# A recurrence's decay sums taken once, with sums, norms and a transposition moved among TensorE's steps

## The reference, cut to what matters

```python
decay = jnp.exp(-jnp.exp(w))
kk = kk * lax.rsqrt(jnp.maximum(jnp.sum(kk * kk, axis=-1, keepdims=True), 1e-24))
k = k * (1 + (a - 1) * k_a)
def step(state, inp):
    r_t, w_t, k_t, v_t, a_t, b_t = inp          # a = -kk, b = kk * a
    sa = jnp.einsum('bhvk,bhk->bhv', state, a_t)
    state = (state * w_t[:, :, None, :] + sa[..., None] * b_t[:, :, None, :]
             + v_t[..., None] * k_t[:, :, None, :])
    y = jnp.einsum('bhvk,bhk->bhv', state, r_t)
    return state, y
```

## Time and profile before

| | us |
|---|---|
| runs of the kernel before, median of 3 | 3309.3 |
| lowest, highest | 3306.87, 3312.51 |
| the profiled execution's own span | 3305.3 |
| TensorE busy in it | 3189.0 (96%) |
| VectorE busy | 2607.8 (79%) |
| ScalarE busy | 1161.1 (35%) |
| GpSimd busy | 2052.8 (62%) |

### The profile page before, as it was taken

One profiled execution on the slowest core, in us unless ns is written; L12 is line 12 of the kernel. 1 busy time (PEld: TensorE's weight loads), 2 busy tenths in 40 slices (PEclk: granted clock), 3 DMA queues, 4 the chain that ended last, 5 costly groups with the idle time before them and its releaser, 6 DMA issues. The chain is left out here.

```text
span 3305.3 us, 57051 instructions
## 1 busy us (share of the span) xinstructions
PE 3189.0 (96%) x21428; PEld 2745.2 (83%) x21428; DVE 2607.8 (79%) x4810; ACT 1161.1 (35%) x1786; POOL 2052.8 (62%) x1304
## 2 busy tenths in 40 slices
PE   8998998899999999999999898999999999999998
PEld 3445887699999999888888777999999998888886
DVE  8583664589998886689899765899988866888997
ACT  0113544233334443333333423333344333333333
POOL 1122444377785655788888603777855568888884
PEclk9999998999999999999999999999999999999999
DMA  9750002377787887999999623777878889999995
GB/s 336 279 207 29 3 4 98 121 255 262 256 280 240 308 323 290 378 348 344 360 352 342 215 83 129 255 265 255 277 249 306 317 296 377 346 347 361 349 342 179
DMA packets 364075, 856.31 MB, mean 259 GB/s; under 512 B 32969, under 2 KB 201393, under 8 KB 355538
## 3 DMA queue, kind: packets, MB, share of 16 engines
q1 hardware_dynamic: 278610, 542.98, 47.3%
q0 software_dynamic: 85248, 310.42, 26.2%
HBM read 750.46 MB, written 102.81 MB: 258 GB/s over the span
## 5 line engine op out<-in xcount | busy, mean ns | idle before, releaser
L1804 PE MATMUL peer_acc<-peer_hhi,peer_uhi 128*128 128x384 f32 x2048 | 697.1, 340 | 8.4 <-POOL peer1same_ulo L2004 4.5
L1804 PE MATMUL peer_acc<-peer_hlo,peer_uhi 128*128 128x384 f32 x2048 | 686.2, 335 | 0.0
L2004 POOL TENSOR_TENSOR peer1same_ulo<-peer_u,peer_uhi 128x1024 fp32r<-128x1024 f32 x128 | 311.7, 2438 | 192.1 <-ACT peer_uhi L1884 190.7
L2004 POOL TENSOR_TENSOR peer0same_ulo<-peer_u,peer_uhi 128x1024 fp32r<-128x1024 f32 x128 | 311.7, 2438 | 191.9 <-ACT peer_uhi L1884 191.1
L1880 ACT ACTIVATE peer_gel<-peer_acc 128x384 f32<-128x384 f32 x256 | 125.7, 491 | 768.9 <-PE peer_acc L1804 768.9
L1804 PEld LDWEIGHTS peer_acc<-peer_hhi,peer_uhi 128*128 128x128 f32 x2048 | 386.3, 189 | 11.4 <-POOL peer1same_ulo L2004 5.8
L1804 PEld LDWEIGHTS peer_acc<-peer_hlo,peer_uhi 128*128 128x128 f32 x2048 | 386.2, 189 | 1.0 <-issue 0.5
L2035 POOL TENSOR_TENSOR peer0lsame_vlo<-peer0l_v,peer0l_vhi 128x1024 fp32r<-128x1024 f32 x128 | 310.3, 2424 | 85.6 <-ACT peer0l_vhi L1919 85.2
L2035 POOL TENSOR_TENSOR peer1lsame_vlo<-peer1l_v,peer1l_vhi 128x1024 fp32r<-128x1024 f32 x128 | 310.2, 2424 | 85.4 <-ACT peer1l_vhi L1919 84.7
L2067 DVE SCALAR_TENSOR_TENSOR peer_acc<-peer_row,peer_p_g,peer_acc 128x1024 f32<-128x1024 f32 x254 | 325.1, 1280 | 36.1 <-DMA peer_row<-in_pe_v,peer_idx 36.1
L1804 PE MATMUL peer_acc<-peer_hhi,peer0same_ulo 128*128 128x384 f32 x1024 | 343.7, 336 | 0.0
(11 more groups left out here) (453 smaller groups left out, 6892.7 us busy)
## 6 DMA issues: line engine op xcount, KB each, us to landing
peer_u<-in_pe_uT SPq DMA_DIRECT2D x256, 512.0 KB, 5.8
peer0l_v<-in_pe_v SPq DMA_DIRECT2D x128, 512.0 KB, 6.0
peer1l_v<-in_pe_v SPq DMA_DIRECT2D x128, 512.0 KB, 6.1
activations<-peer_gel SPq DMA_DIRECT2D x256, 192.0 KB, 6.1
rw_g<-in_ada POOLq DMA_DIRECT2D x60, 512.0 KB, 5.4
routing<-peer0m_wb SPq DMA_DIRECT2D x24, 1024.0 KB, 8.3
peer0l_wt<-routing SPq DMA_DIRECT2D x64, 384.0 KB, 7.5
peer0l_gl<-activations SPq DMA_DIRECT2D x128, 192.0 KB, 7.1
```

The source lines that it names most:

```text
L1804: mm = pe.matmul(ub[e % 2][:, 0:SD], a, h[:, k, 0:SD], start=(n == 0), stop=(n == 3 * KT - 1))
L2004: g.tensor_tensor(ulo[:, q].rearrange("p k e -> p (k e)"), u[:, q].rearrange("p k e -> p (k e)"), uhi[:, e % NH].bitcast(F32).rearrange("p ...
```

## The change

The sums that include the step are kept, 128 columns wide; the exclusive ones are no longer computed. Where AR needs them, ScalarE reads the inclusive ones one column to the left, and a further activation with scale 0 fills the first column. `sum_decay(K, m)` and `spread_norm(K, m)` work on one of the four row tiles; TensorE issues three sums behind level 0 and the fourth inside level 1, between its halves, then three norms behind level 1 and the fourth inside level 2. The transposition b = 1 moves from ahead of level 0 to behind level 3, and ScalarE's copy of it from behind level 0's first copies to behind `decays(K + 1, 1)`. VectorE scales keys and products behind level 2, not level 1. The sums now take bank 3 alone, and the norms bank 2. `cum_done` counts one for a round, and the waits that read it are changed to fit; the waits for `y_done`, `nat_done` and `state_made` in `decays` are as they were.

```diff
--- before
+++ after
@@ -113,7 +113,7 @@
-    for name, n in (("masks", 4 * P), ("sums", 2 * P), ("eye", HALF_P), ("pairs", HALF_P), ("levels", SCAN_LEVELS * HALF_P),
+    for name, n in (("masks", 4 * P), ("sums", P), ("eye", HALF_P), ("pairs", HALF_P), ("levels", SCAN_LEVELS * HALF_P),
@@ -637,7 +637,7 @@
-        cumB = gB[:, 2:4].rearrange("p b (m i q) -> p (b m) i q", m=2, i=2)
+        cumB = gB[:, 3].rearrange("p (m q) -> p m q", q=P)
@@ -689,7 +689,7 @@
-            sp.wait_ge(cum_done, 2 * ROUNDS)
+            sp.wait_ge(cum_done, ROUNDS)
@@ -756,7 +756,7 @@
-                norms = gB[:, 3 if K > 0 else 0].rearrange("p (m q) -> p m q", q=P)
+                norms = gB[:, 2 if K > 0 else 0].rearrange("p (m q) -> p m q", q=P)
@@ -841,7 +841,7 @@
                         invert_deviation(K - 1)
-                    if n == 1 and coming:
+                    if n == 2 and coming:
                         scale_keys(K + 1)
@@ -871,16 +871,17 @@
 
                 r, c, mine = where(K)
                 ms, of = slice(RT // 2 * b, RT // 2 * b + RT // 2), slice(mine.start + RT // 2 * b, mine.start + RT // 2 * b + RT // 2)
-                act.wait_ge(cum_done, 2 * K + (b + 1))
+                act.wait_ge(cum_done, K + 1)
                 if K >= 2:
                     act.wait_ge(y_done, K - 1)
                     act.wait_ge(nat_done, 2 * (K - 1))
                 if K >= 4:
                     act.wait_ge(state_made, K - 3)
-                a.activation(AR[:, of, 0], cumB[:, ms, 1], ACT.Exp, scale=LOG_DECAY, bias=up[:])
-                a.activation(KS[:, of], cumB[:, ms, 0], ACT.Exp, scale=-LOG_DECAY, bias=down[:])
-                a.activation(AR[:, of, 1], cumB[:, ms, 0], ACT.Exp, scale=LOG_DECAY, bias=up[:])
-                a.activation(fac[:, K // 2 % 2, of], cumB[:, ms, 0, P - 1], ACT.Exp, scale=LOG_DECAY).then_inc(exps_made, 1)
+                a.activation(AR[:, of, 0, 0], cumB[:, ms, 0], ACT.Exp, scale=0.0, bias=up[:])
+                a.activation(AR[:, of, 0, 1:P], cumB[:, ms, 0:P - 1], ACT.Exp, scale=LOG_DECAY, bias=up[:])
+                a.activation(KS[:, of], cumB[:, ms], ACT.Exp, scale=-LOG_DECAY, bias=down[:])
+                a.activation(AR[:, of, 1], cumB[:, ms], ACT.Exp, scale=LOG_DECAY, bias=up[:])
+                a.activation(fac[:, K // 2 % 2, of], cumB[:, ms, P - 1], ACT.Exp, scale=LOG_DECAY).then_inc(exps_made, 1)
 
             def take_d(K, n, s):
                 act.wait_ge(d_done, STREAMS * (LV + 1) * K + STREAMS * n + (s + 1))
@@ -911,10 +912,11 @@
                     take_u(K - 1)
+                keeps = past and K - 1 < ROUNDS - 2
                 for s in range(STREAMS):
                     take_d(K, 0, s)
-                    if past and K - 1 < ROUNDS - 2:
-                        take_nat(K - 1, s)
+                    if keeps and s == 0:
+                        take_nat(K - 1, 0)
                 for n in range(LV):
@@ -924,6 +926,8 @@
                         decays(K + 1, 0)
                     if n == 3 and coming:
                         decays(K + 1, 1)
+                    if n == 3 and keeps:
+                        take_nat(K - 1, 1)
                     if not coming:
                         for k in range((KT + LV - 1) // LV * n, min((KT + LV - 1) // LV * (n + 1), KT)):
                             round_wo(k)
@@ -953,22 +957,21 @@
 
-            def sum_decays(K, b):
+            def sum_decay(K, m):
 
                 r, c, mine = where(K)
-                for m in range(RT // 2 * b, RT // 2 * b + RT // 2):
-                    n = RT * r + m
-                    mm = pe.matmul(cumB[:, m].rearrange("p i q -> p (i q)"), rw["s"][:, c, n * P:(n + 1) * P], held["sums"],
-                                   start=True, stop=True)
-                mm.then_inc(cum_done, 1)
-
-            def spread_norms(K):
+                n = RT * r + m
+                mm = pe.matmul(cumB[:, m], rw["s"][:, c, n * P:(n + 1) * P], held["sums"], start=True, stop=True)
+                if m == RT - 1:
+                    mm.then_inc(cum_done, 1)
+
+            def spread_norm(K, m):
 
                 r, c, mine = where(K)
-                for m in range(RT):
-                    mm = pe.matmul(gB[:, 3 if K > 0 else 0, m * P:(m + 1) * P], to_heads[:, RT * r + m], n16[:, c * P:(c + 1) * P],
-                                   start=True, stop=True)
-                mm.then_inc(nb_done, 1)
+                mm = pe.matmul(gB[:, 2 if K > 0 else 0, m * P:(m + 1) * P], to_heads[:, RT * r + m], n16[:, c * P:(c + 1) * P],
+                               start=True, stop=True)
+                if m == RT - 1:
+                    mm.then_inc(nb_done, 1)
 
@@ -1010,7 +1013,7 @@
 
-            def level(K, n):
+            def level(K, n, coming, past):
                 before = STREAMS * LV * K + STREAMS * n
@@ -1021,6 +1024,10 @@
                             mm = pe.matmul(zb[s][other[h], i], m4[part, K % 2, j, part], tt[part, 0, j], start=True, stop=True,
                                            skip_group_check=True)
                     mm.then_inc(z_done, 1)
+                if n == 1 and coming:
+                    sum_decay(K + 1, RT - 1)
+                if n == 2 and coming:
+                    spread_norm(K + 1, RT - 1)
                 for s in range(STREAMS):
                     pe.wait_ge(zs_made, before + (s + 1))
                     for i in range(SH):
@@ -1135,25 +1142,29 @@
                 if past:
                     make_y(K - 1)
                 begin(K, 1)
-                if keeps:
-                    make_nat(K - 1, 1)
                 for n in range(LV):
-                    level(K, n)
+                    level(K, n, coming, past)
                     if n == 0 and coming:
                         if past:
                             pe.wait_ge(yc_made, K)
-                        spread_norms(K + 1)
+                        for m in range(RT - 1):
+                            sum_decay(K + 1, m)
                     if n == 1 and coming:
                         if keeps:
-                            pe.wait_ge(nat_taken, 2 * K)
-                        sum_decays(K + 1, 0)
-                    if n == 2 and coming:
+                            pe.wait_ge(nat_taken, 2 * K - 1)
+                        elif past:
+                            pe.wait_ge(u_taken, K)
+                        for m in range(RT - 1):
+                            spread_norm(K + 1, m)
+                    if n == 3 and keeps:
                         pe.wait_ge(keys_made, K + 2)
-                        sum_decays(K + 1, 1)
+                        make_nat(K - 1, 1)
                 if coming:
                     pe.wait_ge(exps_made, 2 * K + 4)
                 if keeps:
                     make_ds(K - 1)
+                elif coming:
+                    pe.wait_ge(keys_made, K + 2)
                 make_q(K)
                 if coming:
                     first_grams(K + 1)
@@ -1169,9 +1180,10 @@
-            sum_decays(0, 0)
-            sum_decays(0, 1)
-            spread_norms(0)
+            for m in range(RT):
+                sum_decay(0, m)
+            for m in range(RT):
+                spread_norm(0, m)
@@ -2265,7 +2277,7 @@
-    sums = np.concatenate([one(q >= p), one(q > p)], 1)
+    sums = one(q >= p)
```

## The result

| | us |
|---|---|
| changed kernel, median of 5 | 3334.47 (3330.25 to 3337.77) |
| kernel before, median of 5 beside it | 3308.45 (3306.43 to 3312.51) |
| ratio | 1.0077, 95% interval 1.0066 to 1.0088 |
| profiled execution: span | 3332.7 (before 3305.3) |

The change costs 26 us where +15.2 was forecast with a range to 3331: the sign, the place and the mechanism held, the size didn't.

What follows compares the result with a forecast made beforehand. A round was taken to be bound by TensorE up to level 3 and ScalarE just before level 4. Wait 12.0, round 0 and opening sums -0.9 and +0.1, clock 4.0: +15.2 on 3309.3, 3324.5 us, range 3314 to 3331.

Steps and rivals of the forecast that it cites:

- The wait: ScalarE's decays for the next round wait for the moved transposition, holding level 4's copies; loss 2.00 us a round.
- The load stays behind the wait: In ScalarE's decays, the 1.28 us table load begins only after the transposition, at 12.41 us in the round.
- Loss 2.00 us a round: Level 4 starts at 15.57 us in rounds 1 to 6, before at 13.57; 12.0 us for six rounds.
- A3: First half of level 3 on TensorE; forecast to start at 9.39 us in the round, before at 10.76.
- A4: First half of level 4 on TensorE; forecast to start at 15.57 us in the round, before at 13.57.
- The clock: TensorE falls to half clock behind idle 3.2 us ahead of level 4; 1.0 us in four rounds, +4.0.
- Round 0: The round without second transposition or its wait; sums and norms rearranged there, -0.94 us or so.
- Covers: VectorE's keys and products before level 3 (0.26 us spare) and take_nat before make_ds, both costed at nothing.
- A: Rival: the wait holds ScalarE, but the clock stays full in all rounds; +11.2 us, 3320.5, 30%.
- B: Rival: the table load runs ahead of ScalarE's wait, hidden beside level 3; +3.4 us, 3312.7, 5%.
- C: Rival: the transposition doesn't hold ScalarE before level 4; -4.4 us, 3304.9, 11% including a larger form at -9.
- D: Rival: ScalarE must wait out a drain behind each exposed table load; +8.3 us on A, 3328.8, 4%.

Runs made afterwards that it cites:

- e3: Changed kernel with seven filler products of 256 columns behind the second transposition in rounds 1 to 6; 3324.45 us, ratio 1.0044.
- e7: Changed kernel with decays waiting for nat_done first, and four filler products of 256 columns behind the second transposition; 3315.42 us, ratio 1.0020.
- e2: Changed kernel with the order of decays' own waits turned round, nat_done first and cum_done last; 3321.24 us, ratio 1.0035.
- e4: Changed kernel with the exponentials that write KS, and their nat_done wait, moved behind level 4's copies and the other decays; 3307.90 us, ratio 1.0001.

## Why the prediction was wrong

The wait, the exposed load and the place of the idle time were forecast rightly. Two terms of the sum were too small: the loss ahead of level 4 (12.0 us for six rounds, measured 16.5) and the clock (4.0, measured 10.0).

- **The wait** ("decays(K+1, 0) ... waits for 2K"): right. Putting the transposition back, and leaving it but taking the wait off level 4's path, each removes the whole loss.
- **The load stays behind the wait**: right (418.95, behind the transposition), and its price is the step from e3 to e7, both at full clock: 8.4 us in six rounds, or 1.4 a round, of which the load itself is 1.28.
- **"Loss 2.00 us a round"**: the first mis-sized term. At full clock (e3) it was 2.75, so 4.5 us of the missing 10.5 in six rounds. The steps below count from the round's origin, the end of begin(K, 1). In the changed kernel that is 405.83: 396.69, and the 9.14 that lie between the two in the kernel before.
  - A3 came at 9.84, not 9.39. Groups of three take 0.87 and each single one 0.29 (0.42 from 410.40, less the 0.13), where I had 0.81 and 0.14.
  - D3 came 0.17 later again (417.05, after an idle 0.21 put down to VectorE), since the products on VectorE took 1.38 us instead of 1.08. The 1.08 was no fixed price. This instruction took 0.69 in round 0, where GpSimd was idle, 1.08 in rounds 1 to 6 of the kernel before and 1.37 to 1.38 in those of the changed one, where GpSimd had other work at that moment; that the two slow each other was not tested.
  - The load began 0.15 behind the transposition, not 0.06.
  - The added activation took 0.16 (420.25 to 420.41), not 0.05.
  - Together 0.8: A4 at 16.37 instead of 15.57.
- **The clock** ("1.0, in four of the six rounds: +4.0 (bounds 0 and 6 x 1.27 = 7.6)"): the second mis-sized term, and the larger. All six gaps brought half clock, and it cost 10.0 us, 1.67 a round, above my upper bound: the other 6.0 of the 10.5. I had priced one slow stretch by level 0 of round 0; after three of the six gaps (rounds 2, 3 and 6) the slow stretch was about twice as long as after the others (round 3: still 0.50 up to 428), so it ran through level 4, `make_ds` and what follows, and cost 2.0 to 2.3 us. The other three cost 0.9 to 1.4, near the price I had. The rule of the Trainium skill (TensorE: Matmul & The Clock Gate, Why this matters for your kernels), that a gap of this size sets the clock back, agrees with all six gaps; my sum had followed it in four. The shorter gaps here are outside it: 2.00 us in e2 brought half clock four times out of six, and the opening's 2.44, from which I had reasoned that not every gap does so, brought it in the changed kernel.
- **Round 0**: -0.51 instead of -0.94; the same insertions add 0.06 twice and 0.15 twice there too, which is 0.42.
- **The signs of being wrong**: "if A3 isn't 1.4 us earlier in its round" came true. It is 0.92 earlier (9.84 against 10.76), and the two groups of three and the two single products account for the 0.45 that is missing (twice 0.06 and twice 0.15). The place of the load, the idle 0.3 ahead of A3 (0.25) and the 3.2 ahead of A4 (3.4) came as forecast.
- **Covers** (VectorE between levels 2 and 3, take_nat ahead of make_ds): the first failed by 0.17, the second held at full clock (e3: `make_ds` 2.37 behind level 4's start, 2.32 before) and failed in e4.
- **Rivals**: A's full clock is e3, 16.5 us in six rounds where A had 12.0. B was made real by e2 and comes to +13.8 by the medians (+13.7 in rounds 1 to 6; +11.6 by the ratio), not +3.4: the misses above are in it too, and its gap of 2.00 us still brought half clock in four rounds, 5.5 us. Nearest to C is e4, which is no faster. The drain of D does not appear: an activation begins 0.02 us behind the exposed load (418.95+1.28, and 420.25).

## What to carry to other kernels

When work is moved later on one engine, search every semaphore that it raises for waits with an older round's count: the wait stays where it was and may now stand ahead of what the moved work's own engine needs next. A wait that holds the table load holds its 1.28 us too. Price a new idle time on TensorE twice: its length, and a slow stretch behind it, which here cost up to 2.3 us where the nearest one in the trace before had shown 1.27.

## What was not expected of the hardware

Idle times of 2.00 us ahead of level 4 brought half clock after four of six gaps, 3.4 us after all six. The opening's idle 2.44 is the same in all these kernels, yet the sums behind it ran at full clock in the kernel before and at half in the changed one. The table load of an activation ran ahead of the wait that the program wrote first (377.06, with the activation held to 380.03), but stood behind the others (418.95). Two orders of the waits were run, no more.
